# Two two-layer transformer blocks on one core: no semaphore clearing between layers, feed-forward heads that split x*w, the layer-end norm inside the next head

## What is computed

```python
# first block, each of 2 layers
x = x + g_m * mixer1(_rmsnorm(x, norm_mix[l]) * (1 + sc_m) + sh_m)
h = _rmsnorm(x, norm_ffn[l]) * (1 + sc_f) + sh_f
u = _causal_dwconv(h @ ffn_w_up[l], ffn_conv_w[l], ffn_conv_b[l])
ua, uv = jnp.split(u, 2, axis=-1)
x = x + g_f * ((silu(ua) * uv) @ ffn_w_down[l])
# second block, each of 2 layers
h = x + 0.5 * swiglu(rms_norm(x, ffn1_norm[l]), w1, w3, w2)
h = h + mixer2(rms_norm(h, mix_norm[l]), mem)
h = h + 0.5 * swiglu(rms_norm(h, ffn2_norm[l]), w1, w3, w2)
x = rms_norm(h, final_norm[l])
# rms_norm(x, g) = x * rsqrt(mean(x*x) + EPS) * g: a factor per token and one per channel
```

## Time and profile before

| what | us |
|---|---|
| three runs | 2608.2, 2615.17 (median), 2615.4 |
| profiled execution, its own time | 2609.36 |
| its span, first to last instruction | 2607.2 |
| PE busy / PEld busy | 2380.1 / 2014.6 |
| DVE / ACT / POOL busy | 1433.2 / 1043.2 / 84.3 |
| mean granted TensorE clock | 0.949 of full |

### The profile page before, as it was taken

How to read it: one execution, slowest core, us unless ns; L and a number is a source line. 1 busy time by engine, 2 the same in 40 slices (tenths; PEclk the granted TensorE clock), 3 DMA queues, 4 the chain that set the end, 5 groups by cost and what they waited for, 6 DMA issues and landing times. The chain is left out here.

```text
span 2607.2 us, 36697 instructions
## 1 busy us (share of the span) xinstructions
PE 2380.1 (91%) x13638; PEld 2014.6 (77%) x13638; DVE 1433.2 (55%) x2617; ACT 1043.2 (40%) x1849; POOL 84.3 (3%) x97
## 2 busy tenths in 40 slices
PE   6999988899979998898997999978996999978997
PEld 3657777799956677687997998747996899747996
DVE  4796424266624561424766655854654655763654
ACT  2223333065433333304553554343553554443553
POOL 0000001100000000011001000001000000001000
PEclk8999999999999999998998999978998999978999
DMA  8663222335545432233553553203552454203540
GB/s 339 238 243 143 97 97 97 145 146 193 192 147 206 158 113 100 78 139 135 188 192 119 190 193 145 97 25 145 193 193 97 170 187 175 97 25 126 203 181 39
DMA packets 37104, 390.11 MB, mean 150 GB/s; under 512 B 4368, under 2 KB 5008, under 8 KB 5392
## 3 DMA queue, kind: packets, MB, share of 16 engines
q1 hardware_dynamic: 37008, 388.87, 40.3%
HBM read 387.80 MB, written 1.05 MB: 149 GB/s over the span
## 5 line engine op out<-in xcount | busy, mean ns | idle before, releaser
L1083 PE MATMUL bank<-h,ring 128*128 128x256 f32 x2048 | 475.8, 388 | 19.9 <-ACT h L919 14.9
L1083 PEld LDWEIGHTS bank<-h,ring 128*128 128x128 f32 x2048 | 388.6, 193 | 109.7 <-issue 32.7
L605 DVE TENSOR_TENSOR ffn_w_lo<-ring,ffn_w_hi 128x2048 fp32r<-128x2048 f32 x126 | 288.8, 2292 | 168.8 <-ACT ffn_w_hi L554 168.8
L500 PE MATMUL bank<-ffn_hh,ffn_w_hi 128*128 128x512 f32 x1376 | 346.4, 394 | 0.0
L528 PE MATMUL bank<-ffn_g_hi,ffn_w_hi 128*128 128x256 f32 x1056 | 299.3, 283 | 4.5 <-DVE ffn_g_lo L645 4.5
L528 PE MATMUL bank<-ffn_g_lo,ffn_w_hi 128*128 128x256 f32 x1056 | 298.8, 283 | 0.0
L528 PE MATMUL bank<-ffn_g_hi,ffn_w_lo 128*128 128x256 f32 x1056 | 298.8, 283 | 0.0
L500 PEld LDWEIGHTS bank<-ffn_hh,ffn_w_hi 128*128 128x128 f32 x1376 | 249.2, 190 | 44.7
L491 PE MATMUL bank<-ffn_hh,ffn_w_hi 128*128 128x256 f32 x1472 | 216.8, 299 | 65.2 <-ACT ffn_hh L700 64.9
L491 PEld LDWEIGHTS bank<-ffn_hh,ffn_w_hi 128*128 128x128 f32 x1472 | 197.5, 201 | 77.5 <-issue 61.2
L554 ACT ACTIVATE ffn_w_hi<-ring 128x2048 fp32r<-128x2048 f32 x126 | 239.9, 1904 | 1.5 <-issue 0.3
(11 more groups left out here) (251 smaller groups left out, 2910.0 us busy)
## 6 DMA issues: line engine op xcount, KB each, us to landing
ring<-w_in SPq DMA_DIRECT2D x244, 1536.0 KB, 6.3
x<-x_in SPq DMA_DIRECT2D x1, 1024.0 KB, 15.3
mem<-mem_in SPq DMA_DIRECT2D x1, 1024.0 KB, 4.9
y_out<-x SPq DMA_DIRECT2D x1, 1024.0 KB, 3.9
con<-con_in SPq DMA_DIRECT2D x1, 801.0 KB, 7.0
par<-par_in SPq DMA_DIRECT2D x2, 302.0 KB, 19.0
work<-pos_in SPq DMA_DIRECT2D x2, 128.0 KB, 6.2
par<-par_in SPq DMA_DIRECT2D x2, 76.0 KB, 5.4
```

The lines of the kernel that those rows point to most:

```text
L500: pe.matmul(out, w_hi[:, j % 2, c0:c0 + P], hh[:, k, :, :], start=k == 0, stop=False)
L605: dve.tensor_tensor(w_lo[:, j % 2, UP], ring[:, (base + j) % RING, UP], w_hi[:, j % 2, UP], ALU.subtract).then_inc(S(tag + "_up_lo"), 1)
L1083: m = pe.matmul(ps[0:m_rows, 0:T], tile(t0 + k, base)[:, 0:m_rows], rhs, start=k == 0, stop=k == len(src) - 1 and kind != "uk")
```

## The change

1. `clear_all` is gone. Each layer has semaphores of its own name; SyncE clears those of the last layer in the next layer's first block (`clear_stale`), ahead of its own transfers.
2. A plain FFN no longer waits for its norm: `hh` is split from `x * weight` (ScalarE high, VectorE low with one instruction, line 762 of the new code), and the token factor `rs_x` is multiplied onto both up outputs after the add, in two more VectorE instructions per pair. The norm itself runs beside the first pair. `up_pair(1)` waits until `sum_bank` was read.
3. GpSimd casts both halves of the first weights, and does nothing else; VectorE makes all low parts. In a conv head ScalarE adds the shift and casts in one instruction, and the low part is `(h + shift) - high` in one VectorE instruction.
4. The first pair goes hi\*hi of both halves first, then the passes with `w_lo`.
5. The final norm between the layers runs in the head of the next FFN: `x` is scaled chunk by chunk, split, squared and summed there. Only the last one keeps a block, without squares and sums, and its output leaves in four transfers, each as two chunks are ready.
6. `x` is updated as each pair of output chunks is complete (`_acc`), not after the whole last down.
7. The Ln/Exp table set is loaded ahead of the squares at the end of the stage before.

```diff
+        def clear_stale(sp):
+
+            for t in stale["sems"]:
+                sp.sem_clear(t)
...
+            def first_pair():
+
+                for half in range(2):
+                    pe.wait_ge(S(tag + "_first_hi"), half + 1)
+                    if conv:
+                        narrow_pass(0, half, w_hi, 0, half == 0, False, ("_h_hi",))
+                    else:
+                        wide_high(0, half, ("_h_hi", "_h_lo"))
+                        if half == 0 and final:
+                            for k in range(KD):
+                                next_sum(pe, tag + "_in", k)
+                for half in range(2):
+                    pe.wait_ge(S(tag + "_first_lo"), half + 1)
+                    m = narrow_pass(0, half, w_lo, 0, False, False) if conv else wide_low(0, half)
+                if conv:
+                    for half in range(2):
+                        m = narrow_pass(0, half, w_hi, 1, False, True, ("_h_lo",))
+                m.then_inc(S(tag + "_up"), 1)
...
-            up_pair(0, 1, first=True)
-            up_pair(1, 2)
+                    if last and m_ % 2:
+                        mm.then_inc(S(tag + "_acc"), 1)
+                if not last:
+                    mm.then_inc(S(tag + "_down"), 1)
+
+            first_pair()
+            if not conv:
+                pe.wait_ge(S(tag + "_read"), 1)
+            up_pair(1, 1)
             down(0, 1, first=True)
             with pe.Fori(0, (NJ - 2) // 2) as i:
                 for u in range(2):
 
-                    up_pair(u, i * 2 + (u + 3), i * 2 + (u + 1))
+                    up_pair(u, i * 2 + (u + 2), i * 2 + (u + 1))
...
                 else:
 
-                    dve.wait_ge(S(tag + "_part"), n * 2)
                     for half in range(2):
+                        dve.wait_ge(S(tag + "_part"), n * 2 + (half - 1))
                         dst = cv[:, j % 2, half, :]
                         dve.tensor_tensor(dst, up_out(j, half, conv)[:, 0:T], dst,
-                                          ALU.add).then_inc(S(tag + ("_whole" if half else "_whole_a")), 1)
-                    dve.wait_ge(S(tag + "_whole"), n)
+                                          ALU.add).then_inc(S(tag + ("_whole" if half else "_sum_a")), 1)
+                    for half in range(2):
+                        dve.wait_ge(S(tag + ("_whole" if half else "_sum_a")), n)
+                        dst = cv[:, j % 2, half, :]
+                        dve.tensor_tensor(dst, dst, rs_x[:, :],
+                                          ALU.mult).then_inc(S(tag + ("_whole_v" if half else "_whole_a")), 1)
+                    dve.wait_ge(S(tag + "_whole_v"), n)
                 dve.wait_ge(S(tag + "_silu"), n)
                 dve.tensor_tensor(sil[:, j % 2, :], sil[:, j % 2, :], cv[:, j % 2, 1, :], ALU.mult).then_inc(S(tag + "_g"), 1)
...
-                    stream_loop(sp, base + RING, base + NJ + more, S(tag + "_up_lo"), 1, 1, S(tag + "_down_lo"))
+                    stream_loop(sp, base + RING, base + NJ + more, S(tag + "_down_lo"), 1, 1)
...
+
+                        for half in range(2):
+                            unit = slice(half * UNIT, half * UNIT + UNIT)
+                            dve.wait_ge(S(tag + "_first_hi"), half + 1)
+                            dve.tensor_tensor(w_lo[:, 0, unit], ring[:, base % RING, unit], w_hi[:, 0, unit],
+                                              ALU.subtract).then_inc(S(tag + "_first_lo"), 1)
+
...
+                        dve.wait_ge(S(tag + "_z_rs"), 1)
+                        refine(dve, v, sum_bank[:, 0:T], rs_x[:, :], h[:, KD - 1, :], D, S(tag + "_z_read"), 1)
+                        for j in range(KD):
+                            dve.scalar_tensor_tensor(x[:, j, :], x[:, j, :], final(j), rs_x[:, :], ALU.mult,
+                                                     ALU.mult).then_inc(S(tag + "_z_x"), 1)
+                            if j:
+                                low(j - 1)
+                        low(KD - 1)
+                        first_weights_low()
...
+                        for j in range(KD):
+                            low(j)
+                        first_weights_low()
+                    if not conv:
+                        dve.wait_ge(S(tag + "_rs"), 1)
...
 
-                    dve.wait_ge(S(tag + "_down"), NJ)
                     for j in range(KD):
+                        dve.wait_ge(S(tag + "_acc"), j // 2 + 1)
                         dve.scalar_tensor_tensor(x[:, j, :], acc[j // 2][:, j % 2 * T:j % 2 * T + T], finish(j),
...
+                        sp.dma_start(out[:, j:j + 2, :], x[:, j:j + 2, :]).then_inc(S("out_written"), 16)
+                    sp.wait_ge(S("out_written"), 64)
 
                 @block.scalar
                 def _(act):
```

213 lines of the change are left out of this document (109 added, 104 removed).

## The result

The changed kernel takes **2522.84 us** (median of four runs, 2522.31 to 2524.14) against 2612.81 of the kernel before (2608.2 to 2615.4): a ratio of 0.9658, 95% interval 0.9642 to 0.9675, 3.4% faster. The forecast was 2528 with a range of 2508 to 2550. The span of the profiled execution fell from 2607.2 to 2520.5, by 86.7. The table cuts both spans at the same events; a head is measured as in the prediction, from the last sum of squares to the first down matmul.

A forecast was written before the change was run, and what follows sets the result against it. TensorE was taken to bound the plain loops, so only the heads, layer 1's mixer start and the end could shrink much. Terms of 81.9 us off 2609.36 gave 2527.5, forecast 2528, range 2508 to 2550.

The forecast's parts named there:

- Plain heads: Three plain heads, last sum to first down: 16.4 to 19.3 us each, forecast 17.9, saving 26.6 together.
- I take 1.5: Plain heads: allowance in us for a lost clock, which would start the first down 1.2 to 2.9 later.
- VectorE's chain: Plain heads: VectorE's work up to g's low part, with waits and hold, puts the first down 16.4 after the last sum.
- the hold: Heads: GpSimd's casts hold VectorE's first instructions; 1.5 us per plain head, 0.6 in each of the other three.
- TensorE's own way: Plain heads: TensorE's chunks and passes before the first down end at 15.3 us at full clock, just hidden.
- Head with the norm: Head at 2012: 26.8 us against 42.0, saving 15.2, with sums of about 6.1 as the clock falls.
- Conv heads: Two conv heads: 20.7 us from the last sum against 27.2, TensorE's half-clock passes ending them; 13.4 saved together.
- the first rival: Heads: the clock holds and GpSimd holds nothing, 16 us more gained, 2511; chance 14%.
- Tails: Six FFN ends: updating `x` per pair gains 1.15 us each, less 0.4 in four plain ones; 5.3 in all.
- the slower rival: Plain loop: VectorE becomes the bound from 0.66 us per pair beyond the forecast 0.4; 2631 at 1.3 more; chance 3%.
- The other rivals: Heads: clock kept and nothing held, 2511, 14%; or half the gain stays away, 2543 to 2558, 17%.
- the signs of being wrong: TensorE gaps in the plain loop, or longer mixers, which the change leaves alone, would show the prediction wrong.

The follow-up runs named there:

- the second trace: The kernel before the change run once more, unedited; 2609.2 us.
- the trebled version: The changed kernel with the two multiplications by `rs_x` done three times per pair in the plain FFNs; 2582.45 us.

## Why the prediction was right, and where it was off

**The whole.** 2528 against 2522.84. The terms gave 81.9, the edited places gained 91.2, the unedited mixers took 4.4 back. Two errors of opposite sign leave 5 us, and that they met is luck: the terms were 9 short, and the mixers, which had no term, took half of it back.

**Plain heads, forecast 17.9, measured 16.24.** The step that failed is the last one: "I take 1.5" for the clock was added to the 16.4 of VectorE's chain. But the two run side by side, and the later one counts. VectorE's chain ended at 15.3 behind the last sum, 1.1 earlier than summed: the hold was full, as I had it, but laid 1.07 on the chain and not 1.5, and the 0.6 put down for waits between engines did not come. TensorE's own way was 15.19 with the clock kept, close to my 15.3, and lost 1.05 to the clock: 16.24. With the clock kept the head was 15.42 and ended with VectorE; with the hold gone it was 15.05, wherever the clock fell. The lower bound of 16.4, VectorE's chain alone, was therefore 1.0 too high. One more slip lay in the old times: the head at 2382 was taken as a twin of the 25.2 at 1789, but was 24.29, so its saving was forecast 0.9 too large.

**Head with the norm, 26.8 against 25.11.** Hold 0.45 for 0.6, and the sums took 4.70, not 6.1, since the clock came back in their middle (at 1958.0). That TensorE's way and VectorE's chain would come out equal was right: 24.89 and 24.97. That the merging itself would be worth something was never a term, rightly.

**Conv heads, 20.7 against 19.06.** The path that I had end the head, TensorE with its slow first passes, was not the one: with full clock the length is the same within 0.1. Their gain of 16.4 is what the first rival had, but not for its reason, since the clock did fall. It is the largest gain that no run takes apart. What the traces show is that TensorE starts 4.51 behind the last sum instead of 8.32, and that its clock is low for 6.8 us instead of 17.1. The w\_lo passes cost 2.28, not 3.6, because the clock was back by 528. The head is set by VectorE's low parts, ready at 530.1, and the two to three passes behind them.

**Layer 1's mixer, second mixers, the end.** 6.8, 2.5 and 12.0 against 6.8, 2.6 and 12.0. The 5.3 for the clears of a block is confirmed by itself (5.5 to 6.3 with the block's end, where it was removed alone). The other 6.3 at the end, the load gone and a quarter of the output left, was not run by itself. The body of layer 1's mixer, with SyncE's clears now ahead of its transfers, took 458.8 against 459.1, so nothing behind them was late. The Trainium skill, "ScalarE: Activation LUTs", section "What ACT_TABLE_LOAD costs", counts about 2.66 us for a switch of tables, of which 1.38 is the drain. The start of a second mixer gained 1.27, the load alone; no drain shows there, where ScalarE had stood idle for 1.99 ahead of the load.

**Tails.** Forecast 1.15 each (4.12 - 2.9 is 1.22), less 0.4 in plain ones; measured 1.28 and 0.84. The update was worth 1.23 to 1.28 when undone. The 0.4 came out, but as the sum of two: the multiplications cost 0.66 (left out, the last down of a plain FFN starts 0.66 earlier), and the add that no longer waits for both copies gives some 0.3 back.

**The plain loop.** No change, as forecast. The slower rival's point was 0.66 beyond the multiplications' cost and turned out as 0.76. It put each further 0.1 us at 8 us, and the trebled version, 0.56 beyond the point, lost 47.5 in its loops. **The other rivals:** neither the clock nor the hold vanished, and the heads kept all of the gain.

**What had a place only in the range.** The prediction put 6 us for the spread of the runs into its range, and none into its sum. The spread goes with the clock: the runs of before from 2602 to 2611 have a mean granted clock of 0.949 to 0.952, those from 2611.9 to 2616 of 0.947 to 0.948. The profiled one had one of the short first mixers (514.29; 518.68 in the second trace). Longer mixers stood among the signs of being wrong; they were 4.4 longer in the first pair of traces and 2.6 in the second, within what the same code does by itself. Why the clock falls in a mixer where it does, and why this differs after an edit elsewhere by up to 5 us, was not settled.

## What to carry to other kernels

Where two engines work side by side towards one event, estimate each one's end with its own losses and take the later; adding one's loss to the other's end over-prices. Measure slack by adding the same small work once and twice more: nothing happened, then 60 us came, and the two together gave the ring's length. And where a head is a chain of short waits, ask first what clearing, barriers and a wait for a whole tensor cost there; these three made 43 to 50 of the 91 us by the runs that undo them (clearing 23.5, the norm's wait 12 to 19, the update of a whole `x` 7.5), and the arithmetic that was moved into the loop to get rid of the wait cost nothing there and 0.4 in each plain tail.

## What the runs showed of the hardware

- A VectorE instruction of 128x256 with two SBUF inputs that met a GpSimd cast ended 0.27 behind the end of that cast in all four cases of three heads (0.48 became 0.76 and 1.25, 0.42 became 0.88 twice), and GpSimd's cast took 1.23 instead of 1.04 where it met VectorE's: the times of two engines of which each waits for the other's whole instruction. Eight short ones beside 2.22 of casts lost 1.07.
- TensorE's granted clock was low in every plain head of the changed kernel, 4.3 to 7.7 us behind the last sum, after TensorE had stood still for 2.0 and waited for chunks. A burst of matmuls ahead kept it up in the plain and conv heads, not in the longer head with the norm; there it stayed up with one matmul more behind each chunk (sums 3.62 instead of 4.70).
- The same 3.4 us at the lower clock cost a plain head 1.05 of TensorE's time when they lay under passes without waits, and nothing when they lay under waits for chunks (1.7 to 5.1).
- A block in which SyncE clears 84 to 96 semaphores laid 5.5 to 6.3 us on the path; the clears took 5.1 to 5.6 of it, 54 to 60 ns each.
- Two executions of the same program differed by 4.4 and 4.9 us in two mixers, where the granted clock fell at other places.
